# Gate and value strips of the up-projection computed side by side in two PSUM banks

## The chip, the cores and the metric

The kernel runs on one NeuronCore of one Trainium2 chip. The metric is the device time of one execution in microseconds; lower is better. Engines are named as in the profile: PE is TensorE (PEld its weight loads), DVE is VectorE, ACT is ScalarE, POOL is GpSimd, SP is SyncE, which here only issues DMAs.

## The reference, cut to what matters

One layer of a hybrid decoder: a mixer (short convolution and mLSTM), then a ConvGLU feed-forward block, on 272 prompt positions (16 learned ones and 256 given) and 8 sample tokens. The change is in the feed-forward block:

```python
D_MODEL = 2048; D_FF = 11 * D_MODEL // 4        # 5632
h2 = rmsnorm(x, norm2_g)
up, fc = causal_dwconv(h2 @ w_up, fc0, w_ffconv)   # w_up: 2048 x 11264, 3 taps along the sequence
x = x + (jax.nn.silu(up[..., D_FF:]) * up[..., :D_FF]) @ w_down
```

The second half of the columns of `w_up` gives the gate (it goes through silu), the first half gives the value. Everything is fp32.

## The kernel before, in words

**Strips and units.** All products with weights have the same form. A strip is one tile of 128 output columns, accumulated in one PSUM bank over the 16 k-tiles of the input (22 in the down-projection). The activations are the moving operand: 266 columns in the up-projection, 264 in the down-projection. The kernel keeps fp32 accuracy with three products in fp32r: the high part of the weights with the high part of x (`w_hi`, `xh`), high with low (`w_hi`, `xl`), low with high (`w_lo`, `xh`). So a strip of 16 k-tiles is 48 matmuls. Its weights come in two units of 8 k-tiles, 512 KB each: the first half, h = 0, and the second, h = 1.

**The ring.** `w_raw`, `w_hi` and `w_lo` have `RING` = 4 slots of one unit. SP loads unit u + 4 into `w_raw` when the low part of unit u is made (`load`, which waits on `lo_done`). ScalarE makes the high part of unit u + 4 (`split_hi`, L530, which waits for the landing and for `unit_used` of unit u). VectorE makes the low part (`split_lo`, L763, which waits on `hi_done`). TensorE waits on `lo_done` before it begins a unit and adds 1 to `unit_used` at the unit's last matmul. `step(...)` in the streams of ScalarE and VectorE is one such high or low part, always for the unit four further on. All these counters count units in order, and each engine's stream is written out by hand, in order.

**The stages.** The mixer comes first (until about 955 us), then the output projection, then the feed-forward block in two chunks, `c` = 0 and 1. Each chunk has an up-projection stage over 22 tiles f of the hidden layer (`FC` = 22; a gate strip and a value strip each, so 22 pairs) and a down-projection stage over 16 strips, each of 22 k-tiles in units of 8, 8 and 6. The up stages run from about 1045 to 1307 us and from 1440 to 1702 us.

**One pair in the up stage.** The gate strip goes to bank 0 or 2, the value strip to bank 1 or 3 (`q` = 2p + z, z = 0 for the gate). VectorE takes a finished strip from its bank into `zs` (`take`, L772, which multiplies by the normaliser `rbc`), saves its last columns (`up_last`, L1039) and convolves it into `cz` (L1042, L1045, L1049, L1053). ScalarE makes the sigmoid of the gate's `cz` (`sg`, L708), which it waits for on `fconv_step`. GpSimd multiplies `sg` with the gate's `cz` (`gg`, L514), then with the value's `cz` (`hid`, L517). VectorE waits for `hid_done` and splits `hid` into `hh` and `hl` (L1059, L1061), the moving operands of the down-projection. Its first strip waits at k-tiles 0, 11, 20 and 21 for the tiles of `hh` and `hl` that come next.

VectorE's order for one pair before the change: low part, take of the gate, its convolution, low part; low part, take of the value, its convolution, low part; then `hh` and `hl`. ScalarE's order, which the change leaves as it is (L704 to L709):

```python
step(n, 8, u0, 4 * p)
step(n, 8, u0, 4 * p + 1)
step(n, 8, u0, 4 * p + 2)
act.wait_ge(fconv_step, n * 20 + (10 * c * FC + 10 * p + 5))
act.activation(sg[:, :], cz[:, 0, :], ACT.Sigmoid).then_inc(sig_f, 1)
step(n, 8, u0, 4 * p + 3)
```

TensorE runs 48 matmuls for the gate and then 48 for the value. In the second unit of each strip, at its third k-tile, it waits until the strip that last used the next strip's bank is evacuated (`strip`, L1162).

Of the kernel before, what the change touches and what calls it, by code (L numbers as in the profile page):

```python
# [6 lines left out]
def hybrid_decoder_step(nc, ins, outs, scratch_rows, scratch_v):  # L7
# [19 lines left out]
    P = 128  # L27
# [58 lines left out]
    with ctx:  # L86
# [222 lines left out]
        @block.sync  # L309
        def _(sp):  # L310
            x_t = [(0, 0, NMETA, meta), (0, NMETA, P, x_prompt[0, 0:P - NMETA, :]),
                   (1, 0, P, x_prompt[0, P - NMETA:2 * P - NMETA, :]),
                   (2, 0, T2, x_prompt[0, 2 * P - NMETA:SEQ, :]),
                   (2, T2, TL, x_sample[:, 0, :])]
            for h in range(2):
                for j, a, b, src in x_t:
                    c = slice(h * D // 2, (h + 1) * D // 2)
                    sp.dma_start(x_tok[a:b, j, c], src[:, c]).then_inc(x_in[h], 16)
            sp.sem_inc(lo_done, RING)

            def load(u, slot, src, kk):

                sp.wait_ge(lo_done, u + 1)
                sp.dma_start(w_raw[:, slot, 0:kk * P].rearrange("p (k n) -> p k n", k=kk),
                             src).then_inc(unit_landed[slot], 16)

            w_in_v = w_in[0].rearrange("(k p) n -> p k n", p=P)
            w_out_v = w_out[0].rearrange("(k p) n -> p k n", p=P)
            w_up_v = w_up[0].rearrange("(k p) n -> p k n", p=P)
            w_down_v = w_down[0].rearrange("(k p) n -> p k n", p=P)  # L330

            def load_strip(u, i, view, c):
                for h in range(2):
                    load(u + h, (i + h) % RING, view[:, h * KU:(h + 1) * KU, bass.ds(c, P)], KU)

            def front(n):
                for s, c in enumerate((OQ + n * DK, OK + n * DK, OV + n * DV, OV + n * DV + P)):
                    load_strip(n * HEAD_U + 2 * s, 2 * s, w_in_v, c)

            def back(n):  # L340
                for jj in range(2):
                    for s, o in enumerate((OU, OC, OB, OGA, OO, OGB)):
                        load_strip(n * HEAD_U + 8 + 12 * jj + 2 * s, 2 * s, w_in_v, n * DV + o + jj * P)

            front(0)
            with sp.Fori(0, H - 1) as n:
                back(n)
                front(n + 1)
            back(H - 1)
            with sp.Fori(0, KT // 4) as i:  # L350
                for q in range(4):
                    load_strip(i * 8 + (U_B + 2 * q), 2 * q, w_out_v, i * (4 * P) + q * P)
            for c in range(CH):
                u0 = U_C + c * U_CH
                with sp.Fori(1, FC // 2 + 1) as i:
                    for p in range(2):
                        f = i * (2 * P) + (c * FC + p - 2) * P
                        load_strip(i * 8 + (u0 + 4 * p - 8), 0, w_up_v, f + DFF)
                        load_strip(i * 8 + (u0 + 4 * p - 6), 2, w_up_v, f)
                u1 = u0 + 4 * FC  # L360
                with sp.Fori(0, KT // 4) as i:
                    for q in range(4):
                        for h, (k, kk) in enumerate(DOWN_UNITS):
                            load(i * 12 + (u1 + 3 * q + h), (3 * q + h) % RING,
                                 w_down_v[:, c * FC + k:c * FC + k + kk, bass.ds(i * (4 * P) + q * P, P)], kk)

            for h in range(4):
                c = slice(h * D // 4, (h + 1) * D // 4)
                sp.wait_ge(y_done, h + 1)
                sp.dma_start(y_prompt[0, 0:P, c], yt[:, 0, c]).then_inc(stored, 16)  # L370
            sp.wait_ge(y_done, 5)
            sp.dma_start(y_sample[:, 0, :], ys[:, :]).then_inc(stored, 16)
# [387 lines left out]
        def _(v):  # L760
# [265 lines left out]
            for c in range(CH):  # L1026
                u0 = U_C + c * U_CH
                s0 = S_C + c * S_CH
                with v.Fori(0, FC // 2) as n:
                    for p in range(2):  # L1030
                        f = n * 2 + (c * FC + p)
                        for z in range(2):
                            fz = f + (FT if z == 0 else 0)
                            q = 2 * p + z
                            cs = n * 20 + (10 * c * FC + 5 * q)
                            step(n, 8, u0, 2 * q)
                            take(n * 8 + (u0 + 2 * q + 1), q, zs[:, z, :], 0, NM)
                            v.wait_ge(evacuated, out_of(n * 4 + (s0 + q)))
                            v.tensor_scalar(up_last[:, :, bass.ds(fz, 1)].rearrange("p t a -> p (t a)"),  # L1039
                                            zs[:, z, NM - NLAST:NM], 1.0, None, ALU.mult).then_inc(fconv_step, 1)  # L1040
                            wcol = [vecs[:, bass.ds(fz + (6 * KT + t * 2 * FT), 1)] for t in range(CW)]
                            v.tensor_scalar(cz[:, z, :], zs[:, z, 2:NM], wcol[2], None, ALU.mult)\  # L1042
                             .then_inc(fconv_step, 1)
                            v.wait_ge(fconv_step, cs + 2)
                            v.scalar_tensor_tensor(out=cz[:, z, 0:SEQ], in0=zs[:, z, 1:1 + SEQ], scalar=wcol[1],  # L1045
                                                   in1=cz[:, z, 0:SEQ], op0=ALU.mult, op1=ALU.add)\
                                                    .then_inc(fconv_step, 1)
                            v.wait_ge(pre_step, 6)
                            v.tensor_tensor(cz[:, z, SEQ:NF], cz[:, z, SEQ:NF],  # L1049
                                            pre_f[:, bass.ds(fz, 1), :].rearrange("p a b -> p (a b)"), ALU.add)\  # L1050
                             .then_inc(fconv_step, 1)
                            v.wait_ge(fconv_step, cs + 3)
                            v.scalar_tensor_tensor(out=cz[:, z, 0:SEQ], in0=zs[:, z, 0:SEQ], scalar=wcol[0],  # L1053
                                                   in1=cz[:, z, 0:SEQ], op0=ALU.mult, op1=ALU.add)\
                                                    .then_inc(fconv_step, 1)
                            step(n, 8, u0, 2 * q + 1)
                        v.wait_ge(hid_done, f + 1)
                        fl = n * 2 + p
                        v.tensor_scalar(tile_of(hh, fl, 0, NF), hid[:, :], 1.0, None, ALU.mult).then_inc(hid_split, 1)  # L1059
                        v.wait_ge(hid_split, f * 2 + 1)  # L1060
                        v.tensor_tensor(tile_of(hl, fl, 0, NF), hid[:, :], tile_of(hh, fl, 0, NF).bitcast(f32),  # L1061
                                        ALU.subtract).then_inc(hid_split, 1)
                u1 = u0 + 4 * FC
                s1 = s0 + 2 * FC
                if c == 0:
                    with v.Fori(0, KT // 4) as n:
                        for q in range(4):
                            step(n, 12, u1, 3 * q)
                            step(n, 12, u1, 3 * q + 1)
                            v.wait_ge(unit_used, used(n * 12 + (u1 + 3 * q + 2)))  # L1070
                            m = n * 4 + q
                            v.tensor_tensor(tile_of(xres, m, NMETA, NT), bank[q][:, 0:NF], tile_of(xres, m, NMETA, NT),
                                            ALU.add).then_inc(evacuated, 1)
                            step(n, 12, u1, 3 * q + 2)
# [35 lines left out]
        def _(pe):  # L1110
# [168 lines left out]
            turn(aux[3][0:NS * H, 2 * P:3 * P], n_new[:, :, :].rearrange("p b h -> p (b h)"), P)  # L1279
            turn(aux[3][0:H, 3 * P:4 * P], pn_new[:, :], P).then_inc(last_turned, 1)  # L1280

            def up_strip(c, i, q, need=()):
                strip(i * 4 + (S_C + c * S_CH + q), i * 8 + (U_C + c * U_CH + 2 * q), 2 * q, q, xh, xl, 0, NM, need)

            def down_strip(c, i, q, need=(), bank_free=None):

# [7 lines left out]
            for c in range(CH):  # L1294
                if c == 0:

                    pe.wait_ge(acc_done, KT + 1)
                    pe.matmul(aux[0][:, 0:NM], ones[:, :], acc[:, :], start=True, stop=True).then_inc(r2_spread, 1)
                    up_strip(0, 0, 0, tiles_ready(x2g_step, 2, 1, KT))
                    for q in range(1, 4):  # L1300
                        up_strip(0, 0, q)
                with pe.Fori(1 if c == 0 else 0, FC // 2) as i:
                    for q in range(4):
                        up_strip(c, i, q)
                s1 = S_C + c * S_CH + 2 * FC
                hid_need = tiles_ready(hid_split, 2, 2 * c * FC, FC)
                if c == 0:
# [68 lines left out]
```

## Time and profile before

| | |
|---|---|
| median of 3 runs | 1846.76 us (1842.66 to 1850.65) |
| span of the profiled execution, first to last instruction | 1845.5 us |
| TensorE busy | 1788.5 us, 97% |
| VectorE busy | 1093.3 us, 59% |
| ScalarE busy | 746.3 us, 40% |
| GpSimd busy | 396.7 us, 21% |
| HBM read | 312.32 MB, 176 GB/s over the span |

The profile is of one execution. Its own time is the span, 1.3 us under the median of the runs. Times of single instructions are starts from the beginning of the span and durations in us; a number in square brackets is the idle time of the engine before the instruction, and what ended it. Ends of matmuls are modelled, so the distance between starts is what counts for them. A table of stretches gives busy time and instruction count by engine, the granted clock of TensorE as a share of full speed, and the mean busy share of the DMA engines.

### The profile page before, as it was taken

Reading aid. Unit: us, or ns where it says so; the run is one execution under the profiler, and the core shown is the slowest. Engines: PE = TensorE matmul, PEld = TensorE weight load, DVE = VectorE, ACT = ScalarE, POOL = GpSimd, SP = SyncE. Lnnn points to the kernel's source line nnn. Section 1 sums busy time; section 2 is a strip of 40 time slices with the busy share of each in tenths; the row PEclk is TensorE's granted clock in tenths of the full one; section 3 lists DMA queues with packets and bytes.
Section 4 is the critical chain, followed back from the end, with each engine's and each line's share of the span. In section 5 each row is a group of like instructions: output and inputs, shape, how many; then the busy total and the mean of one; then the engine's idle time right before and its main releaser. Section 6 shows DMA issues by size and latency. Waiting matters only on the chain.

```text
span 1845.5 us, 37636 instructions
## 1 busy us (share of the span) xinstructions
PE 1788.5 (97%) x14049; PEld 1769.3 (96%) x14049; DVE 1093.3 (59%) x1792; ACT 746.3 (40%) x864; POOL 396.7 (21%) x322
## 2 busy tenths in 40 slices
PE   6999998999999899999999999999999999999997
PEld 5898998999989899899999999999999999999997
DVE  3664454544546445454567777777655677777554
ACT  6433333333333333333334554445443333333443
POOL 2241321313213131221321122222100222222000
PEclk9999899999999999999999999999999999999999
DMA  7767476575766747667666566666666665565663
GB/s 176 166 195 197 137 200 195 154 199 151 201 194 171 193 138 197 189 170 200 163 199 176 168 175 174 175 179 174 179 178 179 181 179 174 172 179 173 182 174 110
DMA packets 600600, 326.18 MB, mean 177 GB/s; under 512 B 12417, under 2 KB 596609, under 8 KB 599449
## 3 DMA queue, kind: packets, MB, share of 16 engines
q1 hardware_dynamic: 575504, 292.85, 57.9%
q10 hardware_dynamic: 24625, 30.45, 5.0%
q8 instruction: 89, 1.46, 0.3%
q0 software_dynamic: 368, 1.31, 0.2%
q14 instruction: 14, 0.11, 0.0%
HBM read 312.32 MB, written 12.68 MB: 176 GB/s over the span
## 4 chain that ended last, share of the span: by engine, by line
PE 95%; DMA 2%; issue 1%; DVE 1%; ACT 1%; ACTq 0%; POOL 0%; DVEq 0%; POOLq 0%
PE strip L1158 88%; PE aux L1251 2%; PE aux L1240 2%; PE aux L1112 1%; DMA gw<-in_w_in 1%; PE aux L1255 1%; DMA out<-m_samp 1%; DMA rb<-scratch_rows 0%; DVE w_lo L763 0%; PE aux L1129 0%; PE aux L1222 0%; ACT w_hi L530 0%; PE strip L1112 0%; PE aux L1244 0%; ACT yt L749 0%
## 5 line engine op out<-in xcount | busy, mean ns | idle before, releaser
L1158 PE MATMUL strip<-xh,w_hi 128*128 128x266 f32 (+2 forms) x3456 | 999.0, 289 | 29.4 <-issue 19.9
L763 DVE TENSOR_TENSOR w_lo<-w_raw,w_hi 128x1024 fp32r<-128x1024 f32 x560 | 703.6, 1257 | 517.7 <-ACT w_hi L530 515.0
L1158 PE MATMUL strip<-xh,w_lo 128*128 128x266 f32 (+2 forms) x3456 | 996.7, 288 | 0.0
L1158 PE MATMUL strip<-xl,w_hi 128*128 128x266 f32 (+2 forms) x3456 | 995.8, 288 | 0.0
L530 ACT ACTIVATE w_hi<-w_raw 128x1024 fp32r<-128x1024 f32 x560 | 593.0, 1061 | 981.4 <-PE strip L1158 975.2
L1158 PEld LDWEIGHTS strip<-xh,w_hi 128*128 128x128 f32 x3456 | 658.3, 190 | 33.2 <-issue 21.9
L1158 PEld LDWEIGHTS strip<-xl,w_hi 128*128 128x128 f32 x3456 | 657.1, 190 | 0.3
L1158 PEld LDWEIGHTS strip<-xh,w_lo 128*128 128x128 f32 x3456 | 656.5, 190 | 0.0
L1158 PE MATMUL strip<-hh,w_hi 128*128 128x264 f32 x704 | 201.0, 285 | 0.0
L1158 PE MATMUL strip<-hh,w_lo 128*128 128x264 f32 x704 | 200.2, 284 | 0.0
L1158 PE MATMUL strip<-hl,w_hi 128*128 128x264 f32 x704 | 200.0, 284 | 0.0
L514 POOL TENSOR_TENSOR gg<-sg,cz 128x264 f32<-128x264 f32 x44 | 57.3, 1303 | 423.2 <-ACT sg L708 423.2
L1158 PEld LDWEIGHTS strip<-hh,w_hi 128*128 128x128 f32 x704 | 132.6, 188 | 0.3
L1158 PEld LDWEIGHTS strip<-hl,w_hi 128*128 128x128 f32 x704 | 132.7, 189 | 0.0
L1158 PEld LDWEIGHTS strip<-hh,w_lo 128*128 128x128 f32 x704 | 132.5, 188 | 0.0
L517 POOL TENSOR_TENSOR hid<-gg,cz 128x264 f32<-128x264 f32 x44 | 73.8, 1676 | 101.9 <-DVE cz L1053 101.9
L1158 PE MATMUL strip<-mh,w_hi 128*128 128x266 f32 x256 | 73.3, 286 | 0.0
L1158 PE MATMUL strip<-ml,w_hi 128*128 128x266 f32 x256 | 73.2, 286 | 0.0
L1158 PE MATMUL strip<-mh,w_lo 128*128 128x266 f32 x256 | 73.0, 285 | 0.0
L772 DVE TENSOR_TENSOR zs<-strip,rbc 128x266 f32<-128x266 f32 x88 | 38.0, 432 | 29.5 <-PE strip L1158 29.5
L489 POOL TENSOR_TENSOR so<-so,sbm 128x266 f32<-128x266 f32 x16 | 22.7, 1416 | 140.6 <-ACT sbm L659 140.6
L1045 DVE SCALAR_TENSOR_TENSOR cz<-zs,vecs,cz 128x256 f32<-128x256 f32 x88 | 42.7, 485 | 13.0 <-DVE cz L1042 2.1
(253 smaller groups left out, 1208.9 us busy)
## 6 DMA issues: line engine op xcount, KB each, us to landing
w_raw<-in_w_in SPq DMA_DIRECT2D x256, 512.0 KB, 4.2
w_raw<-in_w_up SPq DMA_DIRECT2D x176, 512.0 KB, 3.9
w_raw<-in_w_down SPq DMA_DIRECT2D x64, 512.0 KB, 4.0
w_raw<-in_w_out SPq DMA_DIRECT2D x32, 512.0 KB, 4.3
w_raw<-in_w_down SPq DMA_DIRECT2D x32, 384.0 KB, 3.4
c_st<-in_state_mlstm_C ACTq DMA_DIRECT2D x8, 1024.0 KB, 8.9
vb<-scratch_v ACTq DMA_DIRECT2D x8, 1024.0 KB, 7.8
out<-c_st ACTq DMA_DIRECT2D x8, 1024.0 KB, 8.2
```

What stands on the lines that cost most here:

```text
L489: g.tensor_tensor(so[:, :], so[:, :], sbm[:, :], ALU.mult).then_inc(p_gate, 1)
L514: g.tensor_tensor(gg[:, :], sg[:, :], cz[:, 0, :], ALU.mult).then_inc(gg_done, 1)
L517: g.tensor_tensor(hid[:, :], gg[:, :], cz[:, 1, :], ALU.mult).then_inc(hid_done, 1)
L530: act.activation(w_hi[:, slot, :], w_raw[:, slot, :], ACT.Copy).then_inc(hi_done, 1)
L763: v.tensor_tensor(w_lo[:, slot, :], w_raw[:, slot, :], w_hi[:, slot, :].bitcast(f32), ALU.subtract).then_inc(lo_done, 1)
L772: v.tensor_tensor(out, bank[b][:, 0:width], rbc[:, c0:c0 + width], ALU.mult).then_inc(evacuated, 1)
L1045: v.scalar_tensor_tensor(out=cz[:, z, 0:SEQ], in0=zs[:, z, 1:1 + SEQ], scalar=wcol[1], in1=cz[:, z, 0:SEQ], op0=ALU.mult, op1=ALU.add)\
L1112: return pe.transpose(out, in_, ident[0:k, 0:k])
L1158: mm = pe.matmul(bank[b][:, 0:c1 - c0], wt[:, slot, w], xt[:, k0 + k, c0:c1], start=(first and k == 0 and t == 0), stop=(last and k == kk ...
L1240: pe.matmul(aux[0][:, PM + w * NS + b:PM + w * NS + b + 1], c_st[:, b, w * P:(w + 1) * P], q_t[:, PM + b:PM + b + 1], start=True, stop=True)
L1251: mm = pe.matmul(aux[a][:, q0:PM], lhs, pt[:, c0:c0 + PM - q0], start=(t == 0), stop=(t == 2))
L1255: mm = pe.matmul(aux[3][:, 0:DV + 1], kg[:, t, :], v_tok[:, t, :], start=(t == 0), stop=(t == 2))
```

## The change

Three streams are edited; ScalarE's is not.

- SP: the units of a pair are loaded in the order gate h = 0, value h = 0, gate h = 1, value h = 1 (before: gate h = 0 and 1, value h = 0 and 1). They go to slots 0 to 3 in that order.
- TensorE: `up_pair` takes the place of two `up_strip`s. In each half h it waits for both units, then for each k-tile and each of the three products it issues a matmul for the gate's bank and one for the value's. The last matmul of each strip's half counts the unit as used. The bank waits are one at the start of the pair and one at the third k-tile of the second half.
- VectorE: both low parts of the next pair's first half come ahead of the take of the gate. The other two come each directly behind a take, ahead of that strip's convolution (before: behind the convolution).

```diff
@@ SP
-                        load_strip(i * 8 + (u0 + 4 * p - 8), 0, w_up_v, f + DFF)
-                        load_strip(i * 8 + (u0 + 4 * p - 6), 2, w_up_v, f)
+                        for h in range(2):
+                            for z, col0 in enumerate((f + DFF, f)):
+                                load(i * 8 + (u0 + 4 * p + 2 * h + z - 8), 2 * h + z,
+                                     w_up_v[:, h * KU:(h + 1) * KU, bass.ds(col0, P)], KU)
@@ VectorE
-                            step(n, 8, u0, 2 * q)
-                            take(n * 8 + (u0 + 2 * q + 1), q, zs[:, z, :], 0, NM)
+                            if z == 0:
+                                step(n, 8, u0, 4 * p)
+                                step(n, 8, u0, 4 * p + 1)
+                            take(n * 8 + (u0 + 4 * p + 2 + z), q, zs[:, z, :], 0, NM)
+                            step(n, 8, u0, 4 * p + 2 + z)
                             v.wait_ge(evacuated, out_of(n * 4 + (s0 + q)))
...
-                            step(n, 8, u0, 2 * q + 1)
@@ TensorE
-            def up_strip(c, i, q, need=()):
-                strip(i * 4 + (S_C + c * S_CH + q), i * 8 + (U_C + c * U_CH + 2 * q), 2 * q, q, xh, xl, 0, NM, need)
+            def up_pair(c, i, p, need=()):
+
+                s = i * 4 + (S_C + c * S_CH + 2 * p)
+                u = i * 8 + (U_C + c * U_CH + 4 * p)
+                pe.wait_ge(evacuated, s + 2)
+                for h in range(2):
+                    pe.wait_ge(lo_done, u + 2 * h + 2 + RING)
+                    for k in range(KU):
+                        for at_k, sm, value in need:
+                            if at_k == h * KU + k:
+                                pe.wait_ge(sm, value)
+                        if h == 1 and k == 2:
+                            pe.wait_ge(evacuated, s + 4)
+                        w = slice(k * P, (k + 1) * P)
+                        for t, (wt, xt) in enumerate(((w_hi, xh), (w_hi, xl), (w_lo, xh))):
+                            last = h == 1 and k == KU - 1 and t == 2
+                            for z in range(2):
+                                mm = pe.matmul(bank[2 * p + z][:, 0:NM], wt[:, 2 * h + z, w],
+                                               xt[:, h * KU + k, 0:NM], start=(h == 0 and k == 0 and t == 0), stop=last)
+                                if k == KU - 1 and t == 2:
+                                    mm.then_inc(unit_used, 1)
...
-                    up_strip(0, 0, 0, tiles_ready(x2g_step, 2, 1, KT))
-                    for q in range(1, 4):
-                        up_strip(0, 0, q)
+                    up_pair(0, 0, 0, tiles_ready(x2g_step, 2, 1, KT))
+                    up_pair(0, 0, 1)
                 with pe.Fori(1 if c == 0 else 0, FC // 2) as i:
-                    for q in range(4):
-                        up_strip(c, i, q)
+                    for p in range(2):
+                        up_pair(c, i, p)
```

## Rows read from the trace of the kernel before

**Rows 1.** The page: busy time of TensorE, and the chain that ended last.

```profile
PE 1788.5 (97%) x14049; PEld 1769.3 (96%) x14049; DVE 1093.3 (59%) x1792; ACT 746.3 (40%) x864; POOL 396.7 (21%) x322
...
PE 95%; DMA 2%; issue 1%; DVE 1%; ACT 1%; ACTq 0%; POOL 0%; DVEq 0%; POOLq 0%
PE strip L1158 88%; PE aux L1251 2%; PE aux L1240 2%; PE aux L1112 1%; DMA gw<-in_w_in 1%; PE aux L1255 1%; DMA out<-m_samp 1%; DMA rb<-scratch_rows 0%; DVE w_lo L763 0%; PE aux L1129 0%; PE aux L1222 0%; ACT w_hi L530 0%; PE strip L1112 0%; PE aux L1244 0%; ACT yt L749 0%
```

**Rows 2.** First up stage: length, busy PE, PEld, DVE, ACT, POOL; clock, DMA, GB/s.

```profile
1045.00:1307.00 262.00, 262.00 (x2108) 261.93 (x2109) 204.86 (x394) 130.78 (x136) 59.26 (x45) 1.00 0.60 173
```

**Rows 3.** Timeline of PE in the first up stage: start, duration, instruction.

```profile
1239.21 0.28 PE L1158 MATMUL strip<-xh,w_hi 128*128 128x266 f32 x1
...
1251.01 0.28 PE L1158 MATMUL strip<-xh,w_lo 128*128 128x266 f32 x1
1251.13 0.28 PE L1158 MATMUL strip<-xh,w_hi 128*128 128x266 f32 x1
```

**Rows 4.** Timeline of DVE, from one take of a value strip on.

```profile
1248.35 0.43 DVE L772 TENSOR_TENSOR zs<-strip,rbc 128x266 f32<-128x266 f32 x1 [0.66 <-PE strip L1158]
1248.92 0.18 DVE L1039 TENSOR_SCALAR up_last<-zs 128x10 f32 x1
...
1250.19 0.48 DVE L1053 SCALAR_TENSOR_TENSOR cz<-zs,vecs,cz 128x256 f32<-128x256 f32 x1
1250.60 1.22 DVE L763 TENSOR_TENSOR w_lo<-w_raw,w_hi 128x1024 fp32r<-128x1024 f32 x1
1252.58 0.30 DVE L1059 TENSOR_SCALAR hh<-hid 128x264 f32 x1 [0.76 <-POOL hid L517]
1253.00 0.43 DVE L1061 TENSOR_TENSOR hl<-hid,hh 128x264 f32 x1
1253.35 1.22 DVE L763 TENSOR_TENSOR w_lo<-w_raw,w_hi 128x1024 fp32r<-128x1024 f32 x1
1254.49 0.43 DVE L772 TENSOR_TENSOR zs<-strip,rbc 128x266 f32<-128x266 f32 x1
...
1258.38 1.23 DVE L763 TENSOR_TENSOR w_lo<-w_raw,w_hi 128x1024 fp32r<-128x1024 f32 x1 [0.43 <-ACT w_hi L530]
```

**Rows 5.** Timeline of ACT in the same pair.

```profile
1251.33 1.06 ACT L530 ACTIVATE w_hi<-w_raw 128x1024 fp32r<-128x1024 f32 x1 [1.92 <-PE strip L1158]
...
1257.29 1.06 ACT L530 ACTIVATE w_hi<-w_raw 128x1024 fp32r<-128x1024 f32 x1 [1.92 <-PE strip L1158]
```

**Rows 6.** Timeline of POOL in the same pair.

```profile
1250.76 1.68 POOL L517 TENSOR_TENSOR hid<-gg,cz 128x264 f32<-128x264 f32 x1 [1.76 <-DVE cz L1053]
```

**Rows 7.** All gg and hid: duration in ns, least/median/most.

```profile
L514 POOL TENSOR_TENSOR gg<-sg,cz x44: 752/1482/1562, 1057.5 to 1696.5; 128x264 f32<-128x264 f32 x44
...
L517 POOL TENSOR_TENSOR hid<-gg,cz x44: 1665/1677/1684, 1060.0 to 1700.6; 128x264 f32<-128x264 f32 x44
```

**Rows 8.** Timeline of ACT in the mixer: a table load ahead of a wait.

```profile
105.62 1.28 ACT L653 ACT_TABLE_LOAD   x1
111.99 0.43 ACT L653 ACTIVATE sa<-ga 128x266 f32<-128x266 f32 x1 [5.08 <-DVE ga L772]
112.32 1.99 ACT L530 ACTIVATE w_hi<-w_raw 128x1024 fp32r<-128x1024 f32 x2
```

**Rows 9.** Timeline of DVE: what that activation waited for.

```profile
111.52 0.43 DVE L772 TENSOR_TENSOR ga<-strip,rbc 128x266 f32<-128x266 f32 x1
```

**Rows 10.** Timeline of PE in the mixer, after a wait for a low part.

```profile
636.30 0.39 PE L1158 MATMUL strip<-xh,w_hi 128*128 128x268 f32 x1 [2.44 <-DVE w_lo L763]
636.52 0.28 PE L1158 MATMUL strip<-xl,w_hi 128*128 128x268 f32 x1
```

**Rows 11.** Timeline of DVE: the low part waited for.

```profile
634.98 1.23 DVE L763 TENSOR_TENSOR w_lo<-w_raw,w_hi 128x1024 fp32r<-128x1024 f32 x1 [1.86 <-ACT w_hi L530]
```

**Rows 12.** Timeline of PE: 32 matmuls of one column in the mixer.

```profile
202.73 4.31 PE L1240 MATMUL aux<-q_t,c_st 128*128 128x1 f32 x32
```

**Rows 13.** The page: loads of w_up, count, size, median us to landing.

```profile
w_raw<-in_w_up SPq DMA_DIRECT2D x176, 512.0 KB, 3.9
```

## The prediction

> **What bounds the kernel now.** I read the page's busy shares first: TensorE is busy 97% of the span and the chain that ended last is 95% TensorE, 88% of it the strip matmuls [rows 1]. The table by stage then says that in the first up-projection stage TensorE has no idle time at all, at full granted clock, while VectorE is busy 204.9 of 262 us and the DMA engines 60% [rows 2]. The second stage, 1440 to 1702 us, runs the same code and I take it to be alike. So nothing that the change does can save waiting time in the up-projection; it can only change how long a matmul takes, or bring a wait.
>
> Then I read one pair of strips (value and gate of one tile f) instruction by instruction. The same point of two neighbouring pairs lies 1251.13 - 1239.21 = 11.92 us apart [rows 3]: 96 matmuls of 0.124 us, 24 of them (one unit of weights) in 2.98 us, half a pair in 5.96 us. VectorE spends 4 x 1.22 us of each pair on the low parts, twice 0.43 us on taking a strip from its bank, twice 1.75 us on the convolution (from the start of up_last to the end of the last cz), and waits for GpSimd's hid before it writes hh and hl [rows 4]. That is about 10 of 11.92 us, and it is the engine to watch.
>
> **What the change does, part by part.** The matmuls, weight loads, bytes, evacuations and loads keep their number. What moves is when four things come free.
>
> *TensorE.* A unit was released every 2.98 us, and its replacement (high part on ScalarE, low part on VectorE) had three units, 8.9 us, to be ready. Now a pair has two halves of 5.96 us. Each half needs two units before it begins, and releases two at once. A replacement has only the other half, 5.96 us, as cover.
>
> *The queues behind it.* In ScalarE's order the sigmoid (line 708) stands between the high part of the third unit (the gate's second half, call it hi2) and that of the fourth (hi3). It waits for the gate's convolution. Before, the gate strip was finished half a pair before the value strip, so this convolution was done early. Now both strips end together, and the gate's convolution, the sigmoid, hi3 and the low part lo3 follow each other, and the next pair's second half needs lo3. VectorE's wait for hi3 holds up the value's convolution, and so hid, hh and hl behind it.
>
> I count from X = 0, the moment at which the next pair's first matmul would start without a wait.
> - The gate's last matmul now starts 0.25 us before X. In the trace ScalarE starts 0.32 us after the last matmul of a unit started (1251.01 to 1251.33) [rows 3, 5]. So hi2 and the gate's take start at 0.07.
> - hi2 takes 1.06, ends 1.13; lo2 starts 0.03 later, as 1257.29 + 1.06 to 1258.38 shows [rows 4, 5]: 1.16.
> - The next VectorE instruction starts 1.14 after a low part (1253.35 to 1254.49) [rows 4]: convolution from 2.30 to 4.05.
> - Sigmoid 0.04 after its input (111.52 + 0.43 to 111.99), hi3 0.33 after the sigmoid's start (111.99 to 112.32) [rows 8, 9]: 4.09 and 4.42. hi3 ends 5.48, lo3 runs 5.51 to 6.73.
> - TensorE after a low part: it ended at 636.21, the first matmul is put at 636.30 but the second comes only at 636.52, as if the first had begun at 636.40 [rows 10, 11]: 0.19. The second half can begin at 6.92, and was due at 5.96.
> So this half waits 0.96 us, ends 5.96 later, and there the same chain starts again. It is a loop over one pair: 6.92 + 5.96 = 12.88 us in place of 11.92. The first pair of each stage has no such chain before it, so 2 x 21 = 42 pairs pay: **42 x 0.96 = 40.3 us**.
>
> *The other loop.* The value's convolution starts at 5.51 + 1.14 = 6.65, ends 8.40, hid starts 0.09 later and hh 0.14 after its end (1250.67 to 1250.76, 1252.44 to 1252.58), hl 0.42 after hh, the next low part 0.35 after hl [rows 4, 6]. How long hid takes is a choice. All 44 took 1.68 us, but in the pair shown, as in the others that I read, a low part ran beside it (1250.60 to 1251.82 against 1250.76 to 1252.44) [rows 4, 6, 7]. The like product gg took from 0.75 to 1.56 us [rows 7]; I read the short one as the time alone. In the new order VectorE has nothing left to do but wait for hid, so I take 0.76. Then hid ends 9.25, hh starts 9.39, hl 9.81, lo0 10.16, lo1 11.30, which ends 12.52: the pair after next could start at 12.71, earlier than 12.88, no wait. With 1.68 us it would be 13.63, a wait at the pair's start; but then the second half's wait shrinks by the same time and the period stays 12.88, as long as twice the period is more than 13.63 + 11.92. So the period doesn't hang on this choice.
>
> *Leaving a stage.* The down-projection's first strip needs the last hl at its k-tile 21, 21 x 3 x 0.124 = 7.8 us after X. Before, hl ended 1253.00 + 0.43 = 1253.43 with X at 1248.15 (the take at 1248.35, less 0.32 - 0.12), that is at 5.3: covered by 2.5 us. Now it ends 10.24, TensorE goes on at 10.43: 2.6 us of waiting in each of two stages, **5.2 us**; with the long hid 3.5 each, 7.0 us.
>
> The Trainium skill, page "SBUF — State Buffer", section "Who interferes with whom", says that a VectorE instruction with two SBUF inputs contends with GpSimd's reads, as VectorE's second port pair is shared. The trace agrees (gg 0.75 alone, hid 1.68 beside a low part); by it hid is short in the new order, and the sum has 5.2 rather than 7.0 for the two exits.
>
> *Parts at nothing.* The loads go out in the new order, one behind each low part. lo0 and lo1 end at 11.4 and 12.5, so two loads follow each other by 1.1 us; at a median of 3.9 us to landing [rows 13] the later is there at 16.4 and is wanted after the next first half, 12.88 + 5.96 = 18.8: hidden by over 2 us. The loads of slots 2 and 3 follow at 2.4 and 6.7 and have longer. TensorE's bank wait at k-tile 2 of a second half asks for the last pair's value strip, which is taken by 4.4 (start 3.98, the convolution's 2.30 and 1.68, and 0.43) and wanted at 7.7: hidden by 3 us; the wait at a pair's start asks for strips one pair older. ScalarE's table load stands before the sigmoid's wait: at 105.62 it ran at once, while the sigmoid waited until 111.99 for its input [rows 8]. So in the new order it runs from 1.14 to 2.42, ahead of 4.09: hidden.
>
> *The matmul itself.* No row alternates strip matmuls between two banks. The nearest are 32 matmuls of one column with changing weights, 4.31 us, 0.13 us each [rows 12]: as slow as those of 266 columns. So the weight side, which doesn't change, sets 0.124, and I take that. Bounds: 266 columns at 2.4 GHz, 0.111 us, and the 0.135 us of those rows.
>
> **Sum.** 40.3 + 5.2 = 45.5 us on a span of 1845.5: 1891. The median of the runs lies 1.3 us above that span, so the prediction is **1892 us**.
>
> **Rivals.**
> 1. *Faster matmuls in two banks.* At 0.111 us a half is 5.33 and the period 6.92 + 5.33 = 12.25, +0.33 a pair, 14 us over 42 pairs, less 1.3 us for each of the two first pairs, plus the 5.2 us of the exits: 1863. Chance 0.05. For the other side, not slower than before, 48 matmuls must fit into 11.92 - 6.92 = 5.0 us, which is 0.104 us each; there the loop costs nothing, the two first pairs give back 3.8 of the exits' 5.2, and the kernel ends at 1848; below 0.104 it is faster. Less than the 0.111 us that the columns take at the full clock: 0.03.
> 2. *The chain is shorter than its rows.* Six gaps between engines and overlaps inside VectorE make it up; 0.3 us less in their sum takes 13 us off, 1879. Against it stands that each comes from a row, and that the order of both queues is written out: 0.08.
> 3. *Table load behind the wait.* Then sigmoid and hi3 are 1.28 us later in the pairs that have one, 11 in the first stage: 14 us, 1906. The row at 105.62 speaks against: 0.06. The Trainium skill, page "ScalarE: Activation LUTs", section "What ACT_TABLE_LOAD costs", puts a switch at about 2.66 us with its drain; no drain follows the load before the sigmoid in the stage's rows, and by that figure this rival would cost 29 us.
> 4. *Slower matmuls.* 0.135 us each: 48 x 0.011 = 0.53 more for the waiting half, 42 times, 22 us, 1914: 0.04.
> 5. *Late weights.* Two loads close together landing 2.5 us later than the median would reach hi1; each further us costs up to 42 us: 1900 to 1930: 0.04.
> The forecast has the remaining 0.70, with a range of its own of 1884 to 1901 (0.15 us a pair and the two hid times).
>
> **Numbers.** Within 0.5% (9 us) is about what a measurement of this kernel can't tell from no change. Faster 0.02, same 0.03, slower 0.95. The range that leaves out the two ends of the rivals is 1880 to 1907.
>
> **What would show it.** In the profile after: pairs 12.9 us apart, with an idle TensorE of about 1 us in the middle of each pair put down to w_lo, and none or little at its start; lo3 starting 5.5 us after the take of the gate, behind an idle VectorE that waits for ScalarE; hid at 0.76 us; matmuls 0.124 us apart; one wait of 2.6 us for hl in the first down strip of each stage. The prediction is wrong if the matmul spacing differs, if the sigmoid starts later than 0.1 us after the gate's convolution, or if the wait sits on DMA.

## The result and the profile after

The changed kernel takes 1888.44 us (median of 4 runs, 1881.94 to 1895.16), the kernel before 1847.95 us in the same comparison: ratio 1.0218, 95% interval 1.0187 to 1.025. It is slower, by 40.5 us in the medians. The forecast was 1892 us with a range of 1880 to 1907.

The profiled execution is the fastest of the four, with a span of 1879.9 us against 1845.5 before. Where the time went is read from the starts of the matmuls, first those of w_up, then those of the down-projection (duration in ns, then first and last start in us):

```profile
L1303 PE MATMUL strip<-xh,w_hi x1408: 280/285/480, 1035.5 to 1727.5; 128*128 128x266 f32 x176
...
L1162 PE MATMUL strip<-hh,w_hi x704: 278/283/587, 1315.6 to 1866.1; 128*128 128x264 f32 x176
```

The first up stage begins at 1035.5 and ends at 1315.6, 280.1 us; before it went from 1045.3 to 1307.7, 262.4 us. With the starts at which the second up stage begins and ends in both traces (1436.2 and 1697.8 before, 1448.1 and 1728.1 after), the table is:

| stretch | before, us | after, us | difference |
|---|---|---|---|
| all ahead of the up stages | 1045.3 | 1035.5 | -9.8 |
| first up stage | 262.4 | 280.1 | +17.7 |
| first down stage | 128.5 | 132.5 | +4.0 |
| second up stage | 261.6 | 280.0 | +18.4 |
| second down stage and the end | 147.7 | 151.8 | +4.1 |

The edited part and what follows it grew by 44.2 us. The first line is the mixer and the output projection, whose code is the same in both; it came out 9.8 us shorter in this execution. Over the profiled executions of all eight kernels of this document, which share that part, it ends between 1035.5 and 1046.6, so it varies by itself. The medians, 40.5 us apart, lie nearer to the 44.2.

In the table of waits of TensorE, with its weight loads, from the first up stage on (us in total, times, longest), before there was none of a strip. After:

```profile
PEld strip L1303 <- DVE w_lo L765: 35.4, 42, 0.9
...
PEld strip L1162 <- DVE hl L1065: 5.1, 2, 2.5
```

42 waits for a low part and 2 for hl: as many, and for what, as the forecast had. Where in the pair they fall is seen in the timeline of PE over two pairs:

```profile
1245.72 0.51 PE L1303 MATMUL strip<-xh,w_hi 128*128 128x266 f32 x2 [0.62 <-DVE w_lo L765]
1258.46 0.52 PE L1303 MATMUL strip<-xh,w_hi 128*128 128x266 f32 x2 [0.62 <-DVE w_lo L765]
1271.23 0.52 PE L1303 MATMUL strip<-xh,w_hi 128*128 128x266 f32 x2 [0.62 <-DVE w_lo L765]
```

One wait a pair, 12.74 and 12.77 us apart, where [rows 3] had 11.92. These are the starts of second halves: 1258.46 comes 6.7 us after 1251.75, where the pair began. The chain to it stands in the timelines of ACT and DVE (answering to [rows 4, 5]):

```profile
1251.82 1.06 ACT L532 ACTIVATE w_hi<-w_raw 128x1024 fp32r<-128x1024 f32 x1 [4.09 <-PE strip L1303]
1252.90 1.28 ACT L710 ACT_TABLE_LOAD   x1
1255.78 0.42 ACT L710 ACTIVATE sg<-cz 128x264 f32<-128x264 f32 x1 [1.59 <-DVE cz L1058]
1256.11 1.04 ACT L532 ACTIVATE w_hi<-w_raw 128x1024 fp32r<-128x1024 f32 x1
```

```profile
1251.82 0.44 DVE L774 TENSOR_TENSOR zs<-strip,rbc 128x266 f32<-128x266 f32 x1 [0.29 <-PE strip L1303]
1252.91 1.23 DVE L765 TENSOR_TENSOR w_lo<-w_raw,w_hi 128x1024 fp32r<-128x1024 f32 x1 [0.66 <-ACT w_hi L532]
1254.06 0.17 DVE L1044 TENSOR_SCALAR up_last<-zs 128x10 f32 x1
...
1255.26 0.48 DVE L1058 SCALAR_TENSOR_TENSOR cz<-zs,vecs,cz 128x256 f32<-128x256 f32 x1
1255.66 0.43 DVE L774 TENSOR_TENSOR zs<-strip,rbc 128x266 f32<-128x266 f32 x1
1257.18 1.23 DVE L765 TENSOR_TENSOR w_lo<-w_raw,w_hi 128x1024 fp32r<-128x1024 f32 x1 [1.09 <-ACT w_hi L532]
...
1260.99 0.30 DVE L1063 TENSOR_SCALAR hh<-hid 128x264 f32 x1 [0.98 <-POOL hid L519]
```

The reader is to follow the hand-over: high part at 1251.82, low part at 1252.91, convolution 1254.06 to 1255.74, sigmoid 1255.78, high part 1256.11, low part 1257.18 to 1258.41, TensorE 1258.46. While ScalarE waits 1.59 us for the convolution, VectorE later waits 1.09 us for ScalarE: each is idle in the middle of the other's work. The table load ran at 1252.90, ahead of the sigmoid's wait. GpSimd's two products (answering to [rows 7]) are short now, since VectorE waits beside them:

```profile
L516 POOL TENSOR_TENSOR gg<-sg,cz x44: 752/756/761, 1052.1 to 1732.6; 128x264 f32<-128x264 f32 x44
...
L519 POOL TENSOR_TENSOR hid<-gg,cz x44: 740/755/762, 1055.9 to 1736.4; 128x264 f32<-128x264 f32 x44
```

The last wait of each stage brings something that was not foreseen. In the timeline of PE in the first down strip, and in the table by stretch (us; busy time and count of PE, PEld, DVE, ACT, POOL; granted clock; DMA share; GB/s):

```profile
1325.73 0.59 PE L1162 MATMUL strip<-hh,w_hi 128*128 128x264 f32 x1 [2.31 <-DVE hl L1065]
...
1326.34 0.42 PE L1162 MATMUL strip<-hh,w_lo 128*128 128x264 f32 x1
1326.56 0.42 PE L1162 MATMUL strip<-hh,w_hi 128*128 128x264 f32 x1
```

```profile
1315.60:1323.00 7.40, 7.40 (x63) 7.40 (x62) 5.22 (x12) 4.33 (x5) 0.75 (x1) 1.00 0.66 192
...
1325.70:1327.00 1.30, 1.27 (x6) 1.27 (x7) 1.30 (x2) 0.21 (x1) 0.00 (x0) 0.50 0.00 0
1327.00:1329.00 2.00, 2.00 (x11) 2.00 (x11) 2.00 (x3) 0.85 (x1) 0.00 (x0) 0.52 0.30 88
1329.00:1331.00 2.00, 2.00 (x18) 2.00 (x18) 0.45 (x1) 0.26 (x1) 0.00 (x0) 1.00 0.80 220
```

After the wait the matmuls come 0.22 us apart in place of 0.12: the granted clock is 0.50, the lower of the two levels, 1.2 GHz, for some 3 us. The 14 matmuls from 1325.73 on take 3.23 us, until the next one starts at 1328.96 in PE's timeline; at 0.122 us each they would take 1.71. That costs 1.5 us, on top of the 2.5 us of the wait, and together they are the 4.0 us of the down stage. Why the clock fell here isn't shown; what the runs have on it stands in the last section.

### The profile page after: what moved, and what is told of

Its sections match the earlier page's. It is cut to its first block, busy times and chain, and to the rows that moved or that the text cites. A ratio compares the mean times of both kernels' runs of the same rounds, so it can differ in the third digit from the quotient of the medians.

```text
span 1879.9 us, 37532 instructions
## 1 busy us (share of the span) xinstructions
PE 1793.5 (95%) x14049; PEld 1764.7 (94%) x14049; DVE 1088.0 (58%) x1792; ACT 738.4 (39%) x864; POOL 330.3 (18%) x322
## 4 chain that ended last, share of the span: by engine, by line
PE 57%; issue 36%; POOL 2%; DMA 2%; DVE 1%; ACT 1%; POOLq 0%; ACTq 0%; DVEq 0%
PE strip L1162 51%; PE aux L1255 2%; POOL gg L516 2%; PE aux L1244 1%; PE aux L1116 1%; DMA gw<-in_w_in 1%; PE aux L1259 1%; DVE w_lo L765 1%; DMA out<-m_samp 0%; DMA rb<-scratch_rows 0%; ACT w_hi L532 0%; PE aux L1133 0%; PE aux L1226 0%; PE strip L1116 0%; POOL hid L519 0%
## 5 line engine op out<-in xcount | busy, mean ns | idle before, releaser
L1162 PE MATMUL strip<-xh,w_hi 128*128 128x266 f32 (+2 forms) x2048 | 595.1, 291 | 27.5 <-issue 14.9
L1162 PE MATMUL strip<-xh,w_lo 128*128 128x266 f32 (+2 forms) x2048 | 592.2, 289 | 0.0
L1162 PE MATMUL strip<-xl,w_hi 128*128 128x266 f32 (+2 forms) x2048 | 591.6, 289 | 0.0
L1162 PEld LDWEIGHTS strip<-xh,w_hi 128*128 128x128 f32 x2048 | 390.5, 191 | 31.6 <-issue 16.8
L1162 PEld LDWEIGHTS strip<-xl,w_hi 128*128 128x128 f32 x2048 | 389.7, 190 | 0.2
L1162 PEld LDWEIGHTS strip<-xh,w_lo 128*128 128x128 f32 x2048 | 389.0, 190 | 0.0
L1303 PE MATMUL strip<-xh,w_hi 128*128 128x266 f32 x1408 | 292.7, 289 | 26.2 <-DVE w_lo L765 26.2
L1303 PE MATMUL strip<-xh,w_lo 128*128 128x266 f32 x1408 | 289.0, 287 | 0.0
L1303 PE MATMUL strip<-xl,w_hi 128*128 128x266 f32 x1408 | 288.3, 286 | 0.0
L1303 PEld LDWEIGHTS strip<-xh,w_hi 128*128 128x128 f32 x1408 | 220.0, 189 | 35.5 <-DVE w_lo L765 35.4
L1303 PEld LDWEIGHTS strip<-xh,w_lo 128*128 128x128 f32 x1408 | 220.5, 189 | 0.0
L1303 PEld LDWEIGHTS strip<-xl,w_hi 128*128 128x128 f32 x1408 | 219.3, 189 | 0.0
L516 POOL TENSOR_TENSOR gg<-sg,cz 128x264 f32<-128x264 f32 x44 | 33.2, 755 | 499.9 <-ACT sg L710 499.9
```

Of the source, the lines that this page charges most:

```text
L516: g.tensor_tensor(gg[:, :], sg[:, :], cz[:, 0, :], ALU.mult).then_inc(gg_done, 1)
L1162: mm = pe.matmul(bank[b][:, 0:c1 - c0], wt[:, slot, w], xt[:, k0 + k, c0:c1], start=(first and k == 0 and t == 0), stop=(last and k == kk ...
L1303: mm = pe.matmul(bank[2 * p + z][:, 0:NM], wt[:, 2 * h + z, w], xt[:, h * KU + k, 0:NM], start=(h == 0 and k == 0 and t == 0), stop=last)
```

## The experiments

Ratios are to the kernel before, each with its 95% interval. The first four kernels have one set of runs of the kernel before to compare with, the last two another, and the changed kernel a third. A distance in medians to the changed kernel is therefore good to several us only. Finer is the stretch from the first matmul of w_up to the end of the span, in each kernel's profiled execution, because it leaves out the varying part ahead:

| kernel | from, us | to, us | stretch, us | against the changed kernel |
|---|---|---|---|---|
| before | 1045.3 | 1845.5 | 800.2 | -44.2 |
| changed | 1035.5 | 1879.9 | 844.4 | |
| ScalarE's order | 1042.8 | 1848.9 | 806.1 | -38.3 |
| VectorE's order | 1042.8 | 1843.0 | 800.2 | -44.2 |
| TensorE's order | 1040.1 | 1840.2 | 800.1 | -44.3 |
| a second sigmoid | 1041.9 | 1900.4 | 858.5 | +14.1 |
| hid later, one product | 1041.9 | 1888.0 | 846.1 | +1.7 |
| hid later, two products | 1046.6 | 1904.3 | 857.7 | +13.3 |

**ScalarE's order.** The high part of the fourth unit ahead of the sigmoid:

```diff
                         step(n, 8, u0, 4 * p + 2)
+                        step(n, 8, u0, 4 * p + 3)
                         act.wait_ge(fconv_step, n * 20 + (10 * c * FC + 10 * p + 5))
                         act.activation(sg[:, :], cz[:, 0, :], ACT.Sigmoid).then_inc(sig_f, 1)
-                        step(n, 8, u0, 4 * p + 3)
```

> The changed kernel with one edit: ScalarE makes the high part of the fourth unit ahead of the sigmoid and of its wait. Loop theory (the second half of a pair waits for gate take, low part, convolution, sigmoid, high part, low part in a row): the chain to the fourth low part shortens from 6.8 to about 5.6 us, less than a half pair (5.96 us), so the pairs come every 11.92 us, hid still takes 0.76 us, and only the wait for the last hl stays, about 1.5 us in each of two stages: 1851 to 1855 us, against 1888 of the changed kernel. Rival, two units per half are too little cover in themselves: the period stays near 12.7 us, 1885. Rival, matmuls in two banks are dearer: unchanged, 1888.

Measured: 1849.24 us, ratio 1.0028 (1.0006 to 1.005). Of the 44.2 us in the stretch 38.3 are gone; the rest is in the waits below and in small delays at the starts of some halves. The median lies 2 us under the expected range. The waits of TensorE:

```profile
PEld strip L1162 <- DVE hl L1065: 3.8, 2, 1.9
...
PEld strip L1303 <- DVE w_lo L765: 1.2, 8, 0.2
```

The 42 waits are 8 short ones, 1.2 us in all; had two units per half been too little cover, long waits would have stayed. The two exits wait 1.9 us each; 1.5 was expected. A part of the difference is in this pair of rows, of POOL and then of DVE:

```profile
1250.41 1.55 POOL L516 TENSOR_TENSOR gg<-sg,cz 128x264 f32<-128x264 f32 x1 [7.92 <-ACT sg L711]
```

```profile
1250.13 1.22 DVE L765 TENSOR_TENSOR w_lo<-w_raw,w_hi 128x1024 fp32r<-128x1024 f32 x1
1251.27 0.73 DVE L1044 TENSOR_SCALAR up_last<-zs 128x10 f32 x1
```

gg begins beside a low part and takes 1.55 us instead of 0.75, and the up_last behind it takes 0.73 us instead of 0.17, ending as gg ends.

**VectorE's order.** ScalarE's order stays; the gate's convolution comes ahead of the low part of the third unit:

```diff
                             take(n * 8 + (u0 + 4 * p + 2 + z), q, zs[:, z, :], 0, NM)
-                            step(n, 8, u0, 4 * p + 2 + z)
+                            if z == 1:
+                                step(n, 8, u0, 4 * p + 3)
...
+                            if z == 0:
+                                step(n, 8, u0, 4 * p + 2)
                         v.wait_ge(hid_done, f + 1)
```

> The changed kernel with one edit on VectorE alone: the gate's convolution comes directly behind its take, ahead of the low part of the third unit; ScalarE keeps its order. Loop theory: sigmoid 1.7 us earlier, fourth low part ends near 5.4 instead of 6.6 us after the pair's end, period 11.92 us, wait for the last hl 0.8 us in each stage: 1849 to 1853 us. Rival, the sigmoid's place on ScalarE alone costs the time: stays near 1888. Rival, two banks or two units per half: stays near 1888.

Measured: 1845.4 us, ratio 0.9987 (0.9968 to 1.0005). The only waits of strips from the first up stage on:

```profile
PEld strip L1165 <- DVE hl L1068: 2.3, 2, 1.1
```

So the sigmoid's place on ScalarE alone isn't the cause; with an earlier convolution it does no harm. And this kernel still runs every up-projection matmul in alternation between two banks, at the time of before. Its first up stage, read from these two rows as in the table of the result, is even a little shorter:

```profile
L1306 PE MATMUL strip<-xh,w_hi x1408: 279/285/483, 1042.8 to 1693.6; 128*128 128x266 f32 x176
...
L1165 PE MATMUL strip<-hh,w_hi x600: 278/284/396, 1303.8 to 1790.0; 128*128 128x264 f32 x150
```

That is 261.0 us against 262.4, because the halves of a pair start 5.93 us apart in PE's timeline where they started 5.96 us apart before. Over both up stages this gives back about as much as the two exits cost, 2.3 us. The expectation had no such term, which is a part of why the median lies 3.6 us under its range.

**TensorE's order within a half.** The gate's 24 matmuls, then the value's 24:

```diff
-                    for k in range(KU):
+                    for z, k in ((z, k) for z in range(2) for k in range(KU)):
...
-                            for z in range(2):
+                            if True:
                                 mm = pe.matmul(bank[2 * p + z][:, 0:NM], wt[:, 2 * h + z, w],
```

> The changed kernel with one edit on TensorE: in each half the gate's 24 matmuls come first and then the value's 24, in place of one by one. Loads, slots, waits and the orders of VectorE and ScalarE stay changed. Loop theory: the gate's bank and units are free 2.98 us earlier, the fourth low part is ready 1.9 us before it is needed, hl ends in time: no wait, period 11.92 us, 1846 to 1850 us. Rival, the order of loads and low parts costs the time: near 1888.

Measured: 1845.62 us, ratio 0.9983 (0.9963 to 1.0003), and no wait of TensorE for a low part or for hl is left in the trace. The order of the loads and both reordered streams are harmless without TensorE's alternation. This edit lets the gate's strip end 2.98 us before the value's, and it frees the gate's units 2.98 us earlier too; it doesn't tell the two apart. The timelines of the changed kernel point at the unit: the take ends at 1252.26, and VectorE then waits 0.66 us for the high part that ScalarE could begin only when the third unit was released.

**A second sigmoid.** The chain made longer where it is said to run:

```diff
                         act.activation(sg[:, :], cz[:, 0, :], ACT.Sigmoid).then_inc(sig_f, 1)
+                        act.activation(rt2[:, 0:NF], cz[:, 0, :], ACT.Sigmoid)
                         step(n, 8, u0, 4 * p + 3)
```

> The changed kernel with a second, unused sigmoid of the same input behind the first (an addition; the results stay). Loop theory: the fourth high part, and with it all behind it, is 0.33 to 0.35 us later, so the period is 12.76 + 0.34 us, 42 times, and the two exits: 1902 to 1904 us. Rival, the period is set by another loop, over hid, hl and the first half's low parts, or by the matmuls: 1888 to 1892 us, with the wait only shifted from the pair's start.

Measured: 1900.8 us, ratio 1.0281 (1.0243 to 1.0319), 12.4 us above the changed kernel (14.1 in the stretch), where 14 to 16 were expected.

```profile
PEld strip L1304 <- DVE w_lo L766: 48.8, 42, 1.2
```

48.8 - 35.4 = 13.4 us in 42 waits, 0.32 us each, for an addition of 0.33 us each (1254.23 to 1254.56 in ACT's timeline): the chain passes it on whole.

**hid later.** One unused product of the same inputs ahead of hid on GpSimd, and then two:

```diff
+                g.tensor_tensor(x3[:, 0, :], gg[:, :], cz[:, 1, :], ALU.mult)
+                g.tensor_tensor(x3[:, 1, :], gg[:, :], cz[:, 1, :], ALU.mult)   # in the second kernel only
                 g.tensor_tensor(hid[:, :], gg[:, :], cz[:, 1, :], ALU.mult).then_inc(hid_done, 1)
```

> The changed kernel with a second, unused product of hid's inputs on GpSimd ahead of hid (an addition; the results stay). hid ends 0.76 us later, so the low parts of the first half are ready 13.3 us after the pair's end in place of 12.5, and the pair after next starts half a microsecond late. Two-loop theory: the wait only moves, some 0.5 us to the start of a pair and 0.35 us left in its middle, the period stays 12.76 us, and only the two exits grow by 0.76 us each: 1889 to 1891 us. Rival, waits add up: 0.5 us more in each of 42 pairs, 1910 us.

Measured: 1889.86 us, ratio 1.0235 (1.019 to 1.028), 1.4 us above the changed kernel (1.7 in the stretch), as expected. The waits, and where they fall:

```profile
PEld strip L1304 <- DVE w_lo L766: 32.7, 81, 0.9
```

```profile
1245.86 0.30 PEld L1304 LDWEIGHTS strip<-xh,w_hi 128*128 128x128 f32 x2 [0.45 <-DVE w_lo L766]
1252.17 0.30 PEld L1304 LDWEIGHTS strip<-xh,w_hi 128*128 128x128 f32 x2 [0.30 <-DVE w_lo L766]
1258.74 0.30 PEld L1304 LDWEIGHTS strip<-xh,w_hi 128*128 128x128 f32 x2 [0.56 <-DVE w_lo L766]
```

The first and the third of these rows start a pair, the second is the middle of one. There are 81 waits in place of 42, one at nearly each half, but 32.7 us in all in place of 35.4: a wait at the start of a pair is taken off the wait in its middle. The up stages last 280.2 and 280.1 us, as in the changed kernel.

> As the kernel with hid twice, with one more such product: hid ends 1.5 us later than in the changed kernel. Two-loop theory: now the loop over two pairs rules, 14.0 us to the start of the pair after next and 11.92 us of matmuls, 12.98 us a pair, 0.22 us more in 42 pairs, and 1.5 us more at each exit: 1899 to 1902 us, all of the wait at the start of the pairs and none in their middle. Rival, the loop through the sigmoid rules alone: 1891 us. Rival, waits add up: 1.3 us more in 42 pairs, 1940 us.

Measured: 1905.61 us, ratio 1.0319 (1.0274 to 1.0365), 17 us above the changed kernel where 11 to 14 were expected. Waits of TensorE, and VectorE's timeline:

```profile
PEld strip L1305 <- DVE w_lo L767: 44.8, 42, 1.3
...
PEld strip L1164 <- DVE hl L1067: 7.8, 2, 3.9
```

```profile
1251.96 2.35 DVE L767 TENSOR_TENSOR w_lo<-w_raw,w_hi 128x1024 fp32r<-128x1024 f32 x2
1254.23 0.43 DVE L776 TENSOR_TENSOR zs<-strip,rbc 128x266 f32<-128x266 f32 x1
1254.62 1.22 DVE L767 TENSOR_TENSOR w_lo<-w_raw,w_hi 128x1024 fp32r<-128x1024 f32 x1
```

All the waits are at the starts of pairs now, and pairs are 12.88 and 13.08 us apart (1241.49, 1254.37 and 1267.45 in PE's timeline). The loop that rules is yet another one, and simpler than the one expected: VectorE goes from the two low parts to the take and to the next low part without any idle time, so its own stream sets the period, with the waits in it for the fourth high part and for hid, which both answer to VectorE's own convolutions. The mean period, 12.98 us, is the one that was expected, for another reason. In the profiled executions the part from the first matmul of w_up to the end of the span takes 857.7 us (1046.6 to 1904.3), in the changed kernel 844.4 (1035.5 to 1879.9): 13.3 us, within what was expected. What the medians have beyond that isn't in the edited part of this trace; where it comes from isn't settled, and with an interval of 0.9% on the ratio, 17 us, it may be scatter.

No version beats the kernel before: the two best can't be told from it. In its up stages TensorE has no idle time [rows 2], so an order of the same matmuls has only the 0.03 us of each half to win there, some 2 us in all, and here the waits at the exits take that back.

## Why the prediction was right

**The loop over one pair.** Right, in mechanism, place and number of waits. Two edits that shorten the chain, on two different engines, and one that ends the gate's strip and frees its units earlier each remove the loss, the first of them all but 5.9 us; one that lengthens it by 0.33 us costs 0.32 us a pair. The size was 0.96 us a pair, 40.3 us; measured are 0.84 us of waiting, 35.4 us, and 36.1 us of stage time. The pairs came 12.75 us apart where 12.88 was forecast, and that 0.13 us has two parts, 0.10 in the chain and 0.03 in the matmuls. The chain from X came out at 6.82 in place of 6.92 (first matmul put at 1258.46, the next two 0.36 us later where 0.25 us is the spacing, so effectively 1258.57, against X at 1251.75). 0.07 us of that is the convolution: 1.68 us from up_last, not 1.75. The 1.75 came from rows in which it follows a take; behind a low part its first instructions follow each other closer. The rest is in the second high part (1.04, not 1.06) and in single hand-overs, 0.16 us from the last low part to TensorE in place of 0.19 the largest. The other 0.03 us is the term of the matmuls: a half was put at 5.96 us, as before, and one in alternation takes 5.93 (the 23 steps of two matmuls from 1251.75 to 1257.42 take 5.67 us). The forecast gave the weight side as the reason for 0.124 us; as the figure moved with the banks, that isn't the whole of it, and the reason isn't shown.

**The other loop.** Right: hid takes 0.76 us, no wait at the start of a pair, and the claim that the period doesn't hang on hid's duration held when hid came 0.76 us later (up stages of the same length; TensorE's waits at the exits 6.4 us in place of 5.1). At 1.5 us later it no longer held, as its condition said, though the loop that then ruled was VectorE's own stream.

**Leaving a stage.** The waits were right, 5.1 us measured for 5.2. What the term lacked is the clock behind them: 1.5 us at each exit, 3 us. It makes up for most of what the loop was overrated by, 40.3 against 36.1 us: 45.5 us were forecast for the stages in which 44.2 were found. So the nearness of 1892 to 1888 is in part luck.

**Parts at nothing.** Right: no wait for DMA or for a bank appears, and the table load lies ahead of the sigmoid's wait.

**The rivals.** Faster or slower matmuls in two banks: neither to an extent that matters; 0.247 us for two, where one bank has 0.248. The forecast had named a different spacing as a sign of being wrong; 0.5% is all it differs by. Table load behind the wait and late weights: not in the trace. A shorter chain: a third of it came true, 0.1 us rather than 0.3.

## What to carry to other kernels

When two products are computed side by side instead of one after the other, look at what finishes together, the results and the buffers that they free: the first one's after-work used to run under the second's matmuls, and its cover is gone. If an engine's order puts a wait for that after-work ahead of work that feeds the busiest engine, the wait closes a loop, and the loop's length, not any engine's busy share, is the period (VectorE was busy 192.8 of the 274 us from 1045 to 1319, nearly all of it in the first up stage). Two ways open it: move the feeding work ahead of the wait, or start the awaited work first.

## What the runs showed of the hardware

- The granted clock fell to half after all eight exit waits of 2.3 us and more: 2.3 us (two in the changed kernel), 2.6 (two with two sigmoids), 3.0 (two with hid one product later) and 3.7 (two with hid two products later), for about 3 us each, and for nearly 6 us after the last of them (0.50 from 1761.6 to 1767.3). It stayed at 1.00 after waits of 1.7 and 0.9 us in the kernels with the edited ScalarE and VectorE orders, and also after one of 2.44 us in the mixer [rows 10], which a stretch of 1.00 from 636.3 to 640.0 in the kernel before shows. So a wait of about 2.4 us may or may not cost the clock; what tells the cases apart stays open.
- GpSimd and VectorE hold each other up in both directions. gg took 0.75 us beside an idle VectorE, 1.55 us where it began 0.3 us into a low part (ScalarE's order edited), 1.21 us where it began 0.6 us into one (VectorE's order edited). The small up_last behind that low part took 0.73 us in place of 0.17. The Trainium skill, page "SBUF — State Buffer", section "Who interferes with whom", has this as an exclusive hold on a shared port pair; these numbers agree for the low part, which has two SBUF inputs.
- Alternating matmuls between two PSUM banks, weights changing every time, costs nothing against staying in one: 48 matmuls of 266 columns take 5.93 us in alternation (changed kernel, VectorE's order edited) and 5.96 us in one bank (kernel before, TensorE's order edited).
